# A two-block transformer kernel on one core: VectorE makes weights' low parts ahead of the head norms, ScalarE loads tables and activates the next mLSTM head earlier

## What is computed

```
u   = modulate(rms_norm(x));  u_c = modulate(rms_norm(ctx))          # 512 and 256 tokens
p   = u @ w_in;  pc = u_c @ w_in                                     # all projections
o   = gated linear attention, 4 heads, both directions               # GLA
h   = mLSTM, 4 heads, both directions:
      q, k = silu(conv3(q, k)) per head;  m = running maximum of the gates
      w_intra = exp(log_intra - m_q) * (q k^T);  key weights, decays = exp(...)
      h = num / max(|den|, exp(-m_q))
y_gla = head_rms_norm(o) * silu(gate);  y_m = head_rms_norm(h) * sigmoid(gate)
y   = sigmoid(g1) * (y_gla @ w_br_gla) + sigmoid(g2) * (y_m @ w_br_mlstm)
x   = x + g * (y @ w_out);  x = x + g' * swiglu(norm(x));  return rms_norm(x)
```

## Time and profile before

| | us |
|---|---|
| median of 3 runs | 2896.67 |
| the 3 runs | 2892.72, 2896.67, 2913.54 |
| the profiled execution | 2887.74 |
| its span, first to last instruction | 2885.9 |
| TensorE busy in it | 2699.2 |
| mean granted clock of TensorE | 0.964 |

### The profile page before, as it was taken

How to read it: one execution, slowest core, us unless ns; L and a number is a source line. 1 busy time by engine, 2 the same in 40 slices (tenths; PEclk the granted TensorE clock), 3 DMA queues, 4 the chain that set the end, 5 groups by cost and what they waited for, 6 DMA issues and landing times.

```text
span 2885.9 us, 36282 instructions
## 1 busy us (share of the span) xinstructions
PE 2699.2 (94%) x14244; PEld 2186.4 (76%) x14244; DVE 1407.8 (49%) x1845; ACT 992.7 (34%) x1670; POOL 856.3 (30%) x669
## 2 busy tenths in 40 slices
PE   6988999999999799999998899898989899999998
PEld 6866788887798577888876766657777588788887
DVE  2748755543336676545424354546443543533332
ACT  5458622222243783222223434422222200222222
POOL 5566623335447454143462100300000011200000
PEclk9999999999999999999999999988998899999999
DMA  6220034545432101455453111111111133233332
GB/s 132 83 61 1 19 92 124 153 128 138 115 104 67 37 1 38 115 148 135 132 143 94 50 40 45 44 30 30 44 44 44 30 96 94 81 110 88 93 90 80
DMA packets 396730, 230.46 MB, mean 80 GB/s; under 512 B 9772, under 2 KB 392876, under 8 KB 396560
## 3 DMA queue, kind: packets, MB, share of 16 engines
q1 hardware_dynamic: 394608, 226.19, 28.3%
q0 software_dynamic: 1952, 1.94, 0.8%
HBM read 226.01 MB, written 2.10 MB: 79 GB/s over the span
## 4 chain that ended last, share of the span: by engine, by line
PE 75%; DVE 9%; ACT 8%; DMA 5%; issue 2%; POOL 0%; SPq 0%; DVEq 0%; ACTq 0%; POOLq 0%
PE ps L836 64%; PE scores L836 9%; DMA raws<-in_w_down 4%; PE ps L978 1%; ACT wH L1830 1%; DVE R L2171 1%; DVE wL L2381 1%; DVE ring_parts L2434 1%; DMA ring<-in_w_in 0%; ACT U L1669 0%; ACT spare L1692 0%; ACT R L1697 0%; DMA R<-in_x 0%; DVE spare L2181 0%; ACT R L1669 0%
## 5 line engine op out<-in xcount | busy, mean ns | idle before, releaser
L836 PE MATMUL ps<-xH,wH 128*128 128x512 f32 x1000 | 395.3, 395 | 5.2 <-DVE xL L2356 4.3
L836 PE MATMUL ps<-xL,wH 128*128 128x512 f32 x1000 | 390.5, 391 | 0.0
L836 PE MATMUL ps<-xH,wL 128*128 128x512 f32 x1000 | 390.1, 390 | 0.0
L1830 ACT ACTIVATE wH<-raws 128x2048 fp32r<-128x2048 f32 (+1 forms) x114 | 193.0, 1693 | 497.2 <-PE ps L836 341.1
L2381 DVE TENSOR_TENSOR wL<-raws,wH 128x2048 fp32r<-128x2048 f32 (+1 forms) x114 | 232.5, 2039 | 256.4 <-ACT wH L1830 255.3
L836 PE MATMUL ps<-ring_parts,U_parts 128*128 128x256 f32 (+2 forms) x2000 | 334.3, 294 | 24.6 <-DVE ring_parts L2238 6.7
L836 PEld LDWEIGHTS ps<-ring_parts,U_parts 128*128 128x128 f32 x2000 | 292.1, 199 | 41.4 <-issue 31.8
L836 PE MATMUL ps<-R 128*64 128x128 f32 (+3 forms) x1688 | 242.7, 333 | 35.4 <-DVE R_parts L2192 7.0
L802 POOL CAST ring_parts<-ring 128x2048 fp32r<-128x2048 f32 x34 | 67.8, 1993 | 687.1 <-DMA ring<-in_w_in 614.4
L729 POOL TENSOR_TENSOR spare<-spare,cvec 128x1024 f32<-128x1024 f32 x64 | 121.9, 1905 | 437.3 <-DMA spare<-in_w_ada 437.3
L836 PEld LDWEIGHTS ps<-R 128*64 128x64 f32 (+2 forms) x1688 | 157.3, 166 | 117.3 <-issue 62.1
(11 more groups left out here) (444 smaller groups left out, 4776.3 us busy)
## 6 DMA issues: line engine op xcount, KB each, us to landing
raws<-in_w_gate_up SPq DMA_DIRECT2D x88, 512.0 KB, 5.5
ring<-in_w_in SPq DMA_DIRECT2D x34, 1024.0 KB, 5.8
spare<-in_w_ada SPq DMA_DIRECT2D x64, 512.0 KB, 4.1
raws<-in_w_down SPq DMA_DIRECT2D x32, 704.0 KB, 6.4
raws<-in_w_ffn_in SPq DMA_DIRECT2D x44, 512.0 KB, 5.2
ring<-in_w_in SPq DMA_DIRECT2D x26, 512.0 KB, 5.4
raws<-in_w_ffn_out SPq DMA_DIRECT2D x16, 704.0 KB, 4.7
ring<-in_w_o SPq DMA_DIRECT2D x12, 448.0 KB, 3.8
```

Source lines behind the costliest of these rows:

```text
L836: return nc.tensor.matmul(o, a, b, start=first, stop=last)
L1830: ap.do(f(wH[:, g % 2, 0:n], raws[:, g % 2, 0:n], ACT.Copy), wh_ready)
```

## The change

It has these parts, all in the second block:

1. `head_norm` begins with `root_table()`, a Sqrt of one column that loads the table while ScalarE waits for `og_ready`. This holds for GLA heads and mLSTM heads.
2. `second_low("qk", NH2 + 1)` goes ahead of the last GLA head's `head_outputs`, and at the end of mLSTM heads 0 and 1 `second_low("qk", ...)` of the head after the next goes ahead of `head_outputs`; at the end of head 2 it is `second_low("gates", 0)`.
3. The exponential of rM comes first of the four and has a semaphore of its own, `max_exp`, for which TensorE's transposes wait; head 0 waits for `rows_exp` in each direction.
4. `activate(h + 1)` moves from the end of a head to its direction 1, between the evacuations of "v" 5 and "gate" 0.
5. In direction 0 ScalarE takes an Exp of one column ahead of the wait for Wm.
6. In the last head `second_low("gates", 1)` and `("branch", 0)` go right behind the first weighing of the keys of direction 0 and 1 (they were behind the outputs of direction 0 and behind the product with KQ of direction 1), and `y_subtract` takes tiles 0 to 3 and 4 to 6 between qi and Wm and tile 7 after the product of direction 1 (it took two tiles after Wm and two after the product in each direction).

```diff
--- before.py
+++ after.py
@@ -384,6 +384,7 @@
         act_step, dve_step, pool_step = sem("act_step"), sem("dve_step"), sem("pool_step")
         setup = sem("setup")
         piece_in = [sem(f"piece_in{i}") for i in range(5)]
+        max_exp = sem("max_exp")
         y_high, y_split, branch_full = sem("y_high"), sem("y_split"), sem("branch_full")
         late_read = {}
         lr_in, gates_in = sem("lr_in"), sem("gates_in")
@@ -1388,7 +1389,7 @@
             run(nxt("q"))
             run(nxt("k", 0))
             run(nxt("k", 1))
-            pp.more(rows_exp, 2)
+            pp.more(max_exp, 2)
             bank = db.fill(pe)
             for d in range(2):
                 for j in range(TT):
@@ -1405,6 +1406,8 @@
                         ins = mm(bank[:, j * P:(j + 1) * P], k_[:, 256 + j * P:256 + (j + 1) * P], q_[:, j * P:(j + 1) * P], True, True)
                     ins.then_inc(a_full, 1)
                 sel = pick[:, h, :]
+                if h == 0:
+                    pp.more(rows_exp)
                 between = nxt("v", (1, 4)[d])
                 job(db, lambda b: b[:, :], [(sel, rWK[d][:, 256:768])])
                 some(between, 3)
@@ -1964,6 +1967,7 @@
                     copy_out(dst[:, a:a + n, :], bank[:, 0:n * P].rearrange("p (a c) -> p a c", a=n), a_free)
 
             def head_norm(scratch):
+                root_table()
                 ap.more(og_ready)
                 for t in range(TT):
                     ap.do(f(scratch, og[:, t, :], ACT.Square, accum_out=ssg[:, t:t + 1]))
@@ -2023,10 +2027,10 @@
             evacuate(NH2, ("k", 0), ("k", 1))
             for d in range(2):
                 ap.more(rows_ready)
+                ap.do(f(rM[d], rM[d], ACT.Exp, scale=-1.0), max_exp)
                 ap.do(f(rWK[d], rWK[d], ACT.Exp))
                 ap.do(f(rWI[d], rWI[d], ACT.Exp))
-                ap.do(f(mrow[:, d, 3, :], mrow[:, d, 2, :], ACT.Exp))
-                ap.do(f(rM[d], rM[d], ACT.Exp, scale=-1.0), rows_exp)
+                ap.do(f(mrow[:, d, 3, :], mrow[:, d, 2, :], ACT.Exp), rows_exp)
                 if d == 0:
                     activate(0)
                     evacuate(NH2 + 1, ("q", 0), ("k", 0), ("k", 1))
@@ -2060,16 +2064,19 @@
                             act.wait_ge(y_ready, 2 * NH2 - 1)
                             y_rounds(0, 4)
                     beside(("v", (1, 4)[d]))
+                    if d == 0:
+                        ap.do(f(unused[:, :], eps[:, :], ACT.Exp))
                     ap.more(wexp_in)
                     ap.do(f(Wm, Wm, ACT.Exp), wexp_ready)
                     keys_by_token(kdtm)
                     if h + 1 == NH2:
                         y_rounds(*((4, KT - 1), (KT - 1, KT + 2))[d])
-                    beside(*((("v", 2), ("v", 3)), (("v", 5), ("gate", 0)))[d])
+                    beside(("v", (2, 5)[d]))
+                    if h + 1 < NH2 and d == 1:
+                        activate(h + 1)
+                    beside((("v", 3), ("gate", 0))[d])
                 head_norm(mlstm_squares)
                 beside(("gate", 1))
-                if h + 1 < NH2:
-                    activate(h + 1)
             y_rounds(KT + 2, KT + 5)
             for m in range(2):
                 ap.do(f(first_gates[m][0], first_gates[m][0], ACT.Sigmoid), gate_ready)
@@ -2592,8 +2599,8 @@
                     vp.do(last, conv_ready if at_ == 772 else None)
 
             rows(0)
+            second_low("qk", NH2 + 1)
             head_outputs(NH2 - 1, 3, Y)
-            second_low("qk", NH2 + 1)
             for a in (0, 513, 514, 771, 772, 1285):
                 vp.do(v.memset(raw[:, a:a + 1], 0.0))
             vp.do(v.memset(head(0)[2][:, :, DV:DV + 1], 1.0))
@@ -2611,27 +2618,27 @@
                     dve.wait_ge(mqk_ready, h + 1)
                 bank = db.take(dve)
                 vp.do(v.scalar_tensor_tensor(kdm[:, 256:768], k_[:, 256:768], scale, bank[:, :], ALU.mult, ALU.mult), d_free)
+                if h + 1 == NH2:
+                    second_low(*(("gates", 1), ("branch", 0))[d])
                 bank = db.take(dve)
                 vp.do(v.tensor_copy(dec[:, d, 0:6], bank[:, 256:262]))
                 vp.do(v.scalar_tensor_tensor(kdm[:, 0:256], k_[:, 0:256], scale, bank[:, 0:256], ALU.mult, ALU.mult), d_free)
                 vp.also(kdm_ready)
                 bank = db.take(dve)
                 vp.do(v.tensor_tensor(qi, q_, bank[:, :], ALU.mult), d_free)
+                if h + 1 == NH2:
+                    y_subtract(*((0, 4), (4, KT - 1))[d])
                 bank = db.take(dve)
                 vp.do(v.tensor_tensor(Wm, bank[:, :].rearrange("p (a c) -> p a c", a=TT), bc(tribias[:, d, :], TT, 1), ALU.add), d_free)
                 vp.also(wexp_in)
-                if h + 1 == NH2:
-                    y_subtract(4 * d, 4 * d + 2)
                 vp.more(wexp_ready)
                 if d == 0:
                     vp.more(kq_ready)
                 vp.do(v.tensor_tensor(SCm, Wm, KQ, ALU.mult), sc_ready)
                 if d == 1 and h + 1 < NH2:
                     second_low("gate", NH2 + h + 1)
-                if h + 1 == NH2:
-                    if d == 1:
-                        second_low("branch", 0)
-                    y_subtract(4 * d + 2, 4 * d + 4)
+                if h + 1 == NH2 and d == 1:
+                    y_subtract(KT - 1, KT)
                 states(mlstm_order(d), STm, DV + 1, lambda c: dec[:, d, c:c + 1])
                 for t in range(TT):
                     bank = db.take(dve)
@@ -2649,22 +2656,17 @@
                     if h > 0:
                         second_low("v", NH2 + h + 1)
                     convolve(h + 1)
-                else:
-                    second_low("gates", 0)
                 for d in range(2):
                     mlstm_outputs(h, d)
-                    if h + 1 == NH2 and d == 0:
-                        second_low("gates", 1)
                 vp.also(og_ready)
                 if h + 1 < NH2:
+                    second_low(*(("qk", NH2 + h + 2) if h + 2 < NH2 else ("gates", 0)))
                     head_outputs(h, 4, YM)
                 else:
                     second_low("branch", 1)
                     y_subtract(KT, KT + 2)
                     head_outputs(h, 4, YM, lambda: y_subtract(KT + 2, KT + 5))
                     y_subtract(KT + 5, 2 * KT)
-                if h + 2 < NH2:
-                    second_low("qk", NH2 + h + 2)
 
             for m in range(2):
                 vp.more(gate_ready)
```

## The result

| | before | after |
|---|---|---|
| median of the runs, us | 2894.69 (4 runs) | 2857.95 (4 runs) |
| lowest and highest | 2891.16, 2913.54 | 2856.17, 2858.32 |
| span of the profiled execution | 2885.9 | 2856.5 |
| TensorE busy in it | 2699.2 | 2691.8 |
| mean granted clock | 0.964 | 0.969 |

The ratio of the times is 0.9859, with a 95% interval of 0.9816 to 0.9902. The forecast was 2859.8 us. So the kernel is faster, by 1.4%, and the time lies 1.9 us from the forecast. That closeness is partly luck, as the profiles will show: the two profiled spans are only 29.4 us apart, where 36.9 was forecast.

What follows compares the result with a forecast made beforehand. TensorE, busy 2699 of 2886 us, was taken as the bound, so only its idling and lowered clock could yield time. Terms 5.3 + 4.1 + 13.6 + 7.8 + 6.1 = 36.9 off the 2896.67 median gave 2859.8 us, range 2844 to 2883.

Steps and rivals of the forecast that it cites:

- Part 1: GLA heads 1 to 3: early Sqrt table load cuts three key-copy waits from 2.69 to 1.41 us; 5.3 us with clock.
- Ahead of head 0: Before mLSTM head 0: 4.4 us low-part wait goes, rM transposes start 4.5 earlier but wait about 7.5; gain 4.1 us.
- With rM first it is 0.04 + 1.28 + 0.02 + 0.84 = 2.2: Before head 0: rM's exponential, table load included, ends 2.2 us after the rows instead of 4.7, 2.5 less.
- rule on the shared port: VectorE and GpSimd lock each other out per instruction; before head 0 a cast could cost 1.5 us, leaving 2.6.
- Ends of heads 0 and 1: mLSTM head ends: idle 1.5 becomes 0.3, 3.63 goes, 1.9 of clock returns; 6.8 us each, 13.6 together.
- rival (c): Early table loads fail because ScalarE loads Sqrt again behind the squares; 10.4 us lost, 2870.2 us; chance 0.05.
- One stretch of 1.7 us cost (2085.5): Half-clock stretch on matmuls with 4 rows of input, no wait ahead; such stretches were assumed to stay.
- Slow stretches with no wait ahead of them: Sign of being wrong: slow-clock stretches stay as long as they were with no wait ahead of them.
- clock above 0.97: Sign of being right: TensorE's granted clock above 0.97.
- Rival (a): Waits go but the clock doesn't recover, because of matmuls with 4 rows; 27.0 us left, 2869.7 us; chance 0.14.
- Head 2 to direction 0 of head 3: Gate 1's product to direction 0's last wait: 25.0 us becomes 17.2, VectorE late behind gates 1; saves 7.8, bounds 6.1 and 10.
- Direction 1 of head 3: The 3.21 us wait for gates 1 goes, with 2.9 of clock, leaving a 1.7 stretch; 6.1, bounds 3.2 and 7.8.

Runs made afterwards that it cites:

- the repeat: The changed kernel run and profiled once more with nothing altered, as base for the other follow-ups: 2860.82 us, ratio 0.9861.

## Why the prediction was right, point by point

**Part 1, 5.3 forecast.** From the anchor to 1872.02 the kernel before took 183.65 us, after 176.70: 7.0, and 5.2 in the repeat. The table loads were sized right, 3 x 1.22. The clock is what differs: the second stretch costs 1.7 instead of 3.4, and the one behind the first wait (1.7) is gone after and back in the repeat. Over all twelve profiles of kernels with this edit the stretch takes 176.7 to 179.7. Of the 7.0, 1.1 went back at once, as the next wait for VectorE grew from 2.85 to 4.86, which I had not named. On the table load this case's rows and the Trainium skill ("ScalarE: Activation LUTs", What ACT_TABLE_LOAD costs) differ: with the load ahead, each wait fell by 1.2 to 1.3, one load, and not by the page's 2.66.

**Ahead of head 0, 4.1 forecast.** Measured 5.65 at the transposes of rM, and 5.3 at the start of head 0, as the queue behind them waits 0.8 instead of 0.5 for VectorE. Here a term was mis-sized, "With rM first it is 0.04 + 1.28 + 0.02 + 0.84 = 2.2". ScalarE's timeline at that place, after:

```profile
1976.69 1.28 ACT L2030 ACT_TABLE_LOAD   x1
1980.74 0.84 ACT L2030 ACTIVATE R<-R 4x768 f32<-4x768 f32 x1 [2.76 <-DVE R L2588]
```

The rows were ready at the end of this VectorE operation:

```profile
1980.03 0.68 DVE L2588 TENSOR_TENSOR R<-R,mrow 4x512 f32<-4x512 f32 x1
```

The load ran before the wait for VectorE, 4 us ahead of its exponential. From the rows to the end of rM's it is 0.87 and not 2.2. The order of the four exponentials, undone, cost 1.5 of the 2.5 that I gave it; the load ahead of the wait, which the kernel owes to evacuations that now finish earlier, is the rest. That the longer wait (6.23) would take the place of what was removed was right, though it is below my 7.5, by the same term.

The Trainium skill's rule on the shared port ("SBUF — State Buffer", SBUF: two separate sides), by which a cast could fall on the end of the rows and cost 1.5 us, changed nothing here. The cast came at 1981.53, behind the rows, and ran beside VectorE's low part:

```profile
1981.53 3.26 POOL L803 CAST ring_parts<-ring 128x2048 fp32r<-128x2048 f32 x1 [11.93 <-DMA ring<-in_w_in]
```

The same cast is 1.9 elsewhere. VectorE's low part had started 0.79 ahead of it and took its usual 2.29; the convolution's first operation, started at 1983.43 while the cast still ran, took 1.64, where the same operation takes 0.55 at 1988.17. So each time the one that started second took longer, as the page's exclusive lock has it, and neither was on TensorE's path.

**Ends of heads 0 and 1, 13.6 forecast.** The waits went as written: 1.55 to 0.35 and 3.63 to none, twice, 9.7, and no lowered clock follows (1.9 each before): 13.5. The early Sqrt holds: no load stands at L1974, so rival (c) fell. Undone one by one, the low part gave its 3.63 twice and the early table 1.28 at each of three ends. **But heads 0 to 2 together gained only 5.3 us in length** (218.5 to 213.2), and in the repeat 2.6, as inside the scans the clock costs 8.5 more than before (20.5 against 15.8 - 3.8 = 12.0; 23.9 in the repeat). The failed step is one that I did not write as a term: "One stretch of 1.7 us cost (2085.5) has no wait ahead of it at all; it falls on matmuls with 4 rows of input, and such stretches stay." They don't stay at their cost: 17.1 to 30.7 in the nine profiles without those waits, 12.0 and 13.7 in the two with them. Slow stretches with no wait ahead of them are what the prediction had named as a sign of being wrong, and its sign "clock above 0.97" didn't come either (0.969 and 0.968). How much of it the change causes and how much is scatter stays open, as direction 1 of head 0 shows above. Rival (a) is half right by this: the clock recovers behind the waits, and is lost again at the 4-row matmuls.

**Head 2 to direction 0 of head 3, 7.8 forecast.** 25.0 became 17.15, forecast 17.2; saved 7.85. The chain is the one written down, first by VectorE's timeline of head 3 after:

```profile
2214.58 2.29 DVE L2441 TENSOR_TENSOR ring_parts<-ring,ring_parts 128x2048 fp32r<-128x2048 f32 x1 [3.66 <-POOL ring_parts L803]
2218.40 0.69 DVE L2499 TENSOR_TENSOR R_parts<-R,R_parts 128x512 fp32r<-128x512 f32 x1
...
2222.80 0.69 DVE L2637 TENSOR_TENSOR R<-R 128x512 f32<-128x512 f32 x1 [0.81 <-ACT R L2070]
```

And by ScalarE's:

```profile
2218.73 1.28 ACT L2068 ACT_TABLE_LOAD   x1
2220.02 0.20 ACT L2068 ACTIVATE unused<-eps 128x1 f32<-128x1 f32 x1
2222.14 0.63 ACT L2070 ACTIVATE R<-R 128x512 f32<-128x512 f32 x1 [1.91 <-DVEq L56]
```

VectorE waits 3.66 for GpSimd, as the forecast said, and the exponential doesn't wait for its table. What each edit is worth in it was not in the forecast, and the runs tell, with one profile for each: the activation 8 us, the early Exp 1.7, the subtractions in front of Wm -1.2.

**Direction 1 of head 3, 6.1 forecast.** Measured 7.4 up to its last wait, 0.9 in the rest of direction 0 and 0.9 behind: the stretch behind the old wait for gates 1 is gone altogether, where I had left 1.7 of it. The run with part 6 undone lost 6.5 net. The last transposes wait 2.46 instead of 3.12, where no gain was forecast.

**The sum.** From the anchor to the last transposes 33.6 us were gained, and 27.4 in the repeat (617.3 - 589.9), against 36.9. What fell short are heads 0 to 2, 5.3 us (2.6 in the repeat) against 13.6, by the clock in the scans. The other parts together gave 28.2 (24.8) against 23.3, more than forecast in head 3 above all. So errors cancel in part in the profiles. More of them cancel in the medians, which differ by 36.7 and, beside the repeat, by 32.2: the forecast set out from the median of before, 8.9 above the profiled execution, of which 5 to 6 are its high clock by the estimate above, and the median after lies only 0.4 below its own profiled execution. That made the total come out nearer than its terms. (The upper bounds of the terms sum to 50.4 and not to 49, with 3.8 + 3 x 3.4 for part 1; nothing hangs on it.)

## What to carry to other kernels

Count a removed wait twice, its length from the row and the clock behind it, but then ask where the clock will fall next. Between two profiles of one kernel it moved the length by 6 us, so judge an edit of 1 to 5 us by intervals between rows at full clock, and not by a total. An edit ahead of the bound engine's restart (here the activation of the next head, 2.8 us of ScalarE) can be worth nearly three times its own length. Dealing small matmuls out among dense ones cost 31 to 34 us in the median here; drawing them closer together than they were was not shown to help.

## What the runs showed of the hardware that was not expected

- TensorE's clock is granted at half for 10.2 us with TensorE busy in all of it, the nearest idle time 0.22 us long and 5.7 us earlier (the window at 2019.6 of after); dealing out the 4-row products among the filler took its cost in three heads from 20.5 to 35.8 us, outside the 17.1 to 30.7 that nine profiles with one order show, and that was the largest effect of any edit in the study. What decides between 1.7 and 5.1 at one place stays open: direction 1 of head 0 had 5.1 in nine profiles and 1.7 in two others whose instructions on TensorE are the same up to there (the low parts behind, the dense products added).
- A table load can run ahead of the wait of its own exponential (1976.69 against 1980.74), and at another place waits with it (2222.72, 3.82 idle ahead of it). Which of the two it is, is to be read in the trace for each place.
- One idle wait of 3.42 us went over into 13.6 us at half clock, 6.2 us of cost (window at 2207.4): nearly twice the wait itself, where the two waits of 3.63 at the heads' ends of before cost 1.9 each. Length of the wait alone doesn't give the clock's price.
